# k and v stored by 128-byte pieces after a block transpose, v read back and rounded at half 30, and four steps moved in a one-core hybrid decoder layer

## What is computed

```
h = rms_norm(x) * g_pre
q, k, v, ga, u, vs, gg = split(h @ w_in)          # 512, 256, 256, 512, 512, 512, 512 columns
att = moba(q, k, v, paged cache)                  # 8 heads of 64, 4 kv heads, blocks of 256 keys
v_ln = group_layer_norm(gelu(vs)) * g_sgu
gm = gelu(u) * (tril(w_spatial) @ v_ln + b_spatial)   # chunks of 128 positions
mix = concat(att * silu(ga), gm * silu(gg))
y = x + rms_norm(mix @ w_out) * g_post
```

## Time and profile before

| | |
|---|---|
| median of 3 runs | 285.07 us (284.63, 285.07, 378.24) |
| profiled execution | 283.96 us, of it 282.2 us from the first to the last instruction |
| mean granted TensorE clock | 0.997 of full |
| busy: TensorE, VectorE, ScalarE, GpSimd | 270.9, 197.1, 155.2, 72.3 us |
| DMA | 43.4 MB, 154 GB/s over the span |

### The profile page before, as it was taken

The page is one execution under the profiler, slowest core; times in us unless marked ns, Lnnn a source line. Parts: engine busy times, 40 slices in busy tenths (PEclk is TensorE's granted clock), DMA queues, the critical chain, the costliest instruction groups (busy, mean ns, idle before and its releaser), DMA issues.

```text
span 282.2 us, 6112 instructions
## 1 busy us (share of the span) xinstructions
PE 270.9 (96%) x2155; PEld 238.1 (84%) x2155; DVE 197.1 (70%) x451; ACT 155.2 (55%) x355; POOL 72.3 (26%) x86
## 2 busy tenths in 40 slices
PE   8999989999999999999899999999899999999992
PEld 3799988998997887999687999998799976767892
DVE  4785886598844425925649789899979894927773
ACT  5974578532693323178885466555364562718621
POOL 4546503300311140233033452433450510000000
PEclk9999999999999999999999999999999999999998
DMA  7968997269897888740445017022007504040043
GB/s 244 327 191 209 263 257 175 74 185 277 243 321 226 268 283 246 240 136 16 150 147 162 2 45 217 1 70 82 0 2 266 201 1 151 0 150 2 19 174 123
DMA packets 37602, 43.39 MB, mean 154 GB/s; under 512 B 2963, under 2 KB 32659, under 8 KB 37572
## 3 DMA queue, kind: packets, MB, share of 16 engines
q1 hardware_dynamic: 36626, 40.25, 47.7%
q0 software_dynamic: 944, 2.75, 3.5%
q10 hardware_dynamic: 2, 0.00, 0.0%
HBM read 39.59 MB, written 3.41 MB: 152 GB/s over the span
## 4 chain that ended last, share of the span: by engine, by line
PE 74%; DVE 12%; ACT 9%; issue 3%; DVEq 0%; POOL 0%; ACTq 0%; POOLq 0%
PE Z L1442 11%; PE Z L1447 11%; PE Z L1443 11%; PE T L1360 3%; PE S L1484 3%; DVE probs L1241 3%; PE O L1583 2%; PE Z L1398 2%; PE O L1519 2%; PE S L1398 2%; PE S L1399 2%; PE Z L1400 2%; PE S L1400 2%; PE Z L1399 2%; DVE pT_lo L1247 2%
## 5 line engine op out<-in xcount | busy, mean ns | idle before, releaser
L1442 PE MATMUL Z<-act_hi,w_hi 128*128 128x288 f32 (+1 forms) x344 | 89.6, 293 | 0.4 <-ACT zvs L856 0.3
L1443 PE MATMUL Z<-act_lo,w_hi 128*128 128x288 f32 (+1 forms) x344 | 88.2, 288 | 0.0
L1442 PEld LDWEIGHTS Z<-act_hi,w_hi 128*128 128x128 f32 x344 | 64.8, 188 | 2.6 <-issue 1.6
L1443 PEld LDWEIGHTS Z<-act_lo,w_hi 128*128 128x128 f32 x344 | 64.8, 188 | 0.0
L691 POOL TENSOR_TENSOR w_lo<-w_raw,w_hi 128x1024 fp32r<-128x1024 f32 x16 | 38.2, 2391 | 62.4 <-ACT w_hi L779 62.4
L1447 PE MATMUL Z<-act_hi,w_lo 128*128 128x256 f32 (+1 forms) x336 | 48.9, 288 | 0.0
L1447 PEld LDWEIGHTS Z<-act_hi,w_lo 128*128 128x128 f32 x336 | 44.8, 188 | 0.0
L779 ACT ACTIVATE w_hi<-w_raw 128x1024 fp32r<-128x1024 f32 x32 | 33.6, 1052 | 17.0 <-DMA w_raw<-in_w_out 9.9
L1010 DVE TENSOR_TENSOR w_lo<-w_raw,w_hi 128x1024 fp32r<-128x1024 f32 x15 | 18.1, 1212 | 16.2 <-ACT w_hi L779 16.2
L923 ACT ACTIVATE probs<-S,nmax 128x128 f32<-128x128 f32 (+3 forms) x32 | 16.6, 524 | 22.8 <-DVE nmax L1231 21.5
L1118 DVE STREAM_TRANSPOSE kT<-k_ring 128x1024 f32<-128x1024 f32 x16 | 19.7, 1237 | 0.7 <-PE S L1484 0.5
(11 more groups left out here) (271 smaller groups left out, 549.7 us busy)
## 6 DMA issues: line engine op xcount, KB each, us to landing
w_raw<-in_w_in SPq DMA_DIRECT2D x11, 1024.0 KB, 7.2
k_ring<-in_cache_k SPq DMA_DIRECT2D x64, 128.0 KB, 3.2
v_ring<-in_cache_v SPq DMA_DIRECT2D x64, 128.0 KB, 4.2
w_raw<-in_w_out SPq DMA_DIRECT2D x8, 512.0 KB, 4.4
x_sb<-in_x_prompt SPq DMA_DIRECT2D x4, 512.0 KB, 6.0
x_res<-in_x_prompt SPq DMA_DIRECT2D x4, 512.0 KB, 4.8
out<-y_sb SPq DMA_DIRECT2D x8, 256.0 KB, 2.0
w_raw<-in_w_in SPq DMA_DIRECT2D x2, 512.0 KB, 6.5
```

Of the source, the lines that this page charges most:

```text
L1442: mm(out, wh[:, k, :], act_hi[:, k, cols], start=(k == 0), stop=False)
L1443: mm(out, wh[:, k, :], act_lo[:, k, cols], start=False, stop=False)
```

## The change

- WB goes from half 7 to 8.
- KVN 0 to 3 go, with kvn. In their place VectorE turns kv32 (k0, k1, v0, v1, each 128 channels x 512 tokens) in place by blocks of 32x32 (KVB 0 to 3 at halves 10, 12, 14, 16). GpSimd then stores each by four DMAs of 32 partitions, 512 pieces of 128 bytes each: v at halves 26 and 27 (KVD 2, 3), k at halves 34 and 35 (KVD 0, 1).
- v is read back from its output: GpSimd waits for the eight v stores at half 28 (VLD) and loads 512 KB into v_tok, over the v part of kv32. At half 30 (VST) ScalarE waits for that load and rounds all of it in one copy, VectorE subtracts once. PPV 0 waits for this.
- The first gg tile (VectorE, half 40) waits for all k and v stores.
- VSN 2, 3 and 4 go from halves 28, 29, 31 to 27, 28, 29, LN from half 32 to 30, where it stands behind VST and ahead of DPT 1 and PSC 0.
- At half 43, SP 0 goes behind PSC 13 and PN 13, and PPV 11 ahead of PTR 12.
- SP waits for x tile 1 before it issues x tiles 2 to 4. The first three halves wait for the four parts of act_hi one k-group at a time.

```diff
-    after(7, ("WB",))
+    after(8, ("WB",))
-    after(16, ("KVN", 4), ("KVN", 0))
-    for n, h in enumerate((17, 20, 22)):
-        after(h, ("KVN", 1 + n))
+    for j in range(4):
+        after(10 + 2 * j, ("KVB", j))
+    after(16, ("KVN", 4))
+    after(26, ("KVD", 2))
+    after(27, ("KVD", 3))
+    after(28, ("VLD",))
+    after(30, ("VST",), ("LN",))
+    after(34, ("KVD", 0))
+    after(35, ("KVD", 1))
-    for n, h in enumerate((24, 25, 28, 29)):
+    for n, h in enumerate((24, 25, 27, 28)):
         after(h, ("VSN", n))
-    after(31, ("VSN", 4))
-    after(32, ("LN",))
+    after(29, ("VSN", 4))
@@ schedule(), per half h
+        if spread == [0]:
+            after(h, ("SP", 0), ("PPV", u - 2), ("PTR", u - 1))
+        else:
@@ SyncE
             load_first(1)
+            sp.wait_ge(x_in[1], 16)
             for tt in (2, 3, 4):
@@ GpSimd
+                elif kind == "KVD":
+                    j = s[1]
+                    out, landed = (k_prompt, stored_k) if j < 2 else (v_prompt, stored_v)
+                    rows = out[0, 0].rearrange("(b j) h d -> j b (h d)", j=32)
+                    pool.wait_ge(kv_turned, j + 1)
+                    for a in range(4):
+                        at = P * (j % 2) + 32 * a
+                        pool.dma_start(rows[:, :, at:at + 32], kv32[32 * a:32 * a + 32, j, 0:SEQ].rearrange("p (b i) -> p b i", i=32))\
+                            .then_inc(landed, 16)
+                elif kind == "VLD":
+                    pool.wait_ge(t_full, T_OF["KVN", 4] + 1)
+                    pool.wait_ge(stored_v, 8 * 16)
+                    pool.dma_start(v_tok[:, :, :], v_prompt[0, 0].rearrange("(t p) h d -> p t (h d)", p=P)).then_inc(v_back, 16)
@@ ScalarE
+                elif kind == "VST":
+                    act.wait_ge(v_back, 16)
+                    nc.scalar.activation(v_st[:, :, :, 0:HD], v_tok[:, :, :].rearrange("p t (h d) -> p t h d", h=KVH), ACT.Copy).then_inc(vst_hi, 1)
@@ VectorE
+                elif kind == "KVB":
+                    j = s[1]
+                    if j < 2:
+                        dve.wait_ge(k_first, 2 * j + 2)
+                    else:
+                        dve.wait_ge(z_free["act"], freed(Z_FREED_BY, HALF_AT[TILE_OF["v", j - 2], 1])[1])
+                    nc.vector.transpose(kv32[:, j, 0:SEQ], kv32[:, j, 0:SEQ]).then_inc(kv_turned, 1)
+                elif kind == "VST":
+                    dve.wait_ge(vst_hi, 1)
+                    nc.vector.tensor_tensor(v_st[:, :, :, HD:], v_tok[:, :, :].rearrange("p t (h d) -> p t h d", h=KVH),
+                                            v_st[:, :, :, 0:HD].bitcast(fp32), ALU.subtract).then_inc(vst_done, 1)
@@ TensorE, first three halves
-                        pe.wait_ge(x_hi, 4)
                         for k in range(KD):
+                            if k % 4 == 0:
+                                pe.wait_ge(x_hi, 3 + k // 4)
                             mm(out, wh[:, k, :], act_hi[:, k, cols], start=(k == 0), stop=False)
```

More of the change, by code:

```diff
@@ L125, in schedule @@
         u = h - first
-        if h in [2 * TILE_OF["gg", gp] + 3 for gp in range(3)]:
-            after(h, ("SP", (h - 3) // 2 - TILE_OF["gg", 0]))
+        spread = [gp for gp in range(3) if h == 2 * TILE_OF["gg", gp] + 3]
+        for gp in (spread if spread != [0] else []):
+            after(h, ("SP", gp))
         if u < len(UNITS):
             after(h, ("PSC", u), ("PN", u))
[L130 to L133, removed]
+        if spread == [0]:
+            after(h, ("SP", 0), ("PPV", u - 2), ("PTR", u - 1))
+        else:
+            if 1 <= u < len(UNITS) + 1:
+                after(h, ("PTR", u - 1))
+            if 2 <= u < len(UNITS) + 2:
+                after(h, ("PPV", u - 2))
         after(h, ("ZE", h // 2, h % 2))
@@ L298, in build @@
         R_V = region(4096 + 8192 + 10240)
-        kvn = place("kvn", [P, 2, 512], fp32, R_V)
+        v_tok = place("v_tok", [P, 4, KVW], fp32, R_Z + 2 * ZB + 2 * TOK * 4)
         ln_sq = place("ln_sq", [P, 512], fp32, R_V)
@@ L411, in build @@
         v_in = [sem(f"v_in{n}") for n in range(4)]
-        stored_kv = [sem("stored_kv0"), sem("stored_kv1")]
+        stored_k, stored_v, v_back, kv_turned = (sem(n) for n in ("stored_k", "stored_v", "v_back", "kv_turned"))
         stored_kvs = sem("stored_kvs")
@@ L649, in _ @@
             sp.wait_ge(stored_sgu, 16)
-            for n in range(2):
-                sp.wait_ge(stored_kv[n], 2 * 32)
+            sp.wait_ge(stored_k, 8 * 16)
+            sp.wait_ge(stored_v, 8 * 16)
             sp.wait_ge(stored_kvs, 32)
@@ L729, in _ @@
                 elif kind == "KVN":
[L730 to L731 removed]
                     pool.wait_ge(t_free["act"], freed(T_FREED_BY, T_OF[s])[1])
[L733 to L735 removed]
+                    pool.dma_start(kv_rows(k_prompt, k_sample, 4), kv_s[:, 0:KVW]).then_inc(stored_kvs, 16)
+                    pool.dma_start(kv_rows(v_prompt, v_sample, 4), kv_s[:, KVW:2 * KVW]).then_inc(stored_kvs, 16)
+                elif kind == "KVD":
[11 more added lines that the diff above has]
+                    pool.dma_start(v_tok[:, :, :], v_prompt[0, 0].rearrange("(t p) h d -> p t (h d)", p=P)).then_inc(v_back, 16)
                 elif kind == "DOT" and s[1] == 1:
@@ L872, in _ @@
                     R = ROWS[tt]
[L873 to L880, removed]
+                    take(n, kv_s[:, 0:512], T[n % 2][0:R, :])
+                elif kind == "VST":
+                    act.wait_ge(v_back, 16)
+                    nc.scalar.activation(v_st[:, :, :, 0:HD], v_tok[:, :, :].rearrange("p t (h d) -> p t h d", h=KVH), ACT.Copy).then_inc(vst_hi, 1)
                 elif kind == "DEX":
@@ L1087, in _ @@
                         if what == "gg" and j == 0 and half == 0:
-                            dve.wait_ge(t_full, T_OF["KVN", 3] + 1)
+                            dve.wait_ge(t_full, T_OF["KVN", 4] + 1)
+                            dve.wait_ge(stored_k, 8 * 16)
+                            dve.wait_ge(stored_v, 8 * 16)
                         nc.vector.scalar_tensor_tensor(dst[:, j, cols], th[:, g % 2, 0:wide], 1.0, bank[:, 0:wide], ALU.add, ALU.mult)\
@@ L1573, in _ @@
                     if u == 0:
-                        pe.wait_ge(vst_done, 4)
+                        pe.wait_ge(vst_done, 1)
                         pe.wait_ge(own_taken, 1)
```

4 lines of the change are left out of this document (removed).

## The result

The changed kernel takes 286.71 us (median of 22 executions, 284.55 to 290.76) against 284.36 us for the kernel before, measured beside it (median of 22). The ratio is 1.0077, 95% interval [1.0053, 1.0101]: 0.8% or 2.2 us slower, which is within 2%, but surely not the small gain that was forecast. The medians in this text are of all executions and the ratios leave out those in the slower state, so a difference of medians and one of ratios need not agree.

The account below looks back on a forecast made before the run. TensorE, busy 96% of the span, was taken as the bound. By half 26 -2.7, half 30 +2.2, LN gone -0.45, SP 0 +0.45 sum to -0.5 us: 284.6 us by the median, range 280.5 to 289.5.

Parts of the forecast that it names:

- WB: Half 7 to 8: moving it closes TensorE's 0.82 us wait for VectorE's copy; gain 0.9 us with the restart.
- The sixteen transposes: KVN 0 to 3 removed: four blocks of 0.44 us go and a 0.33 us wait closes; gain 2.1 us.
- KVB: Halves 10 to 16, VectorE: the first block transpose delays the k_lo of half 11; loss 0.3 us, bounds 0 to 0.8.
- The start: Held x tiles and finer wait on act_hi in the first halves: taken 0, bounds -0.3 to +0.3 us.
- The stores and the way back: Halves 26 to 30: 0.75 us an issue, v back near 132.2 just before ScalarE needs it; cost 0.
- Rival 2: v comes back late at VST and TensorE stops: +2.6 us (287.2) to +6 us (290.6); chance 0.17.
- VSN, VST, LN at half 30: Halves 27 to 31: new work ahead of DPT 1 and PSC 0 delays TensorE; loss 2.2 us, upper bound 3.0.
- the collision: Half 30: VectorE's two-input subtraction for v is held by GpSimd's w_lo; half 32 3.0 us late, 2.3 without it.
- LN gone at half 32: Half 32: a table switch goes and TensorE's 0.42 us wait closes; gain 0.45 us.
- SP 0: Half 43: spatial product behind the scores, its sum later on VectorE; taken +0.45 us, between 0.9 lost and nothing.
- rival 3: Order changes in halves 30 and 43 cost their upper bounds, +0.8 and +0.45 us more: 285.9, up to 287; chance 0.10.

Follow-up runs that it names:

- e4: The kernel before with the start alone changed (x tiles held, finer wait, WB at half 8): 283.43 us, ratio 0.9977.
- e6: The kernel before with only the new order of half 43 (spatial product behind scores, product with v ahead of transposes): 286.81 us, ratio 1.0064.
- e11: The kernel before with only the first spatial product moved behind the scores in half 43: 288.24 us, ratio 1.0141.
- e10: The kernel before with only the product with v moved ahead of the transposes of probabilities in half 43: 284.12 us, ratio 0.9998.
- e9: e5 with the four KVB transposes at halves 12, 13, 14 and 16: 282.23 us, ratio 0.9913.
- e1: The changed kernel with x tiles 2 to 4 issued at once, not held: 287.96 us, ratio 1.0151.
- e3: The changed kernel with VSN and LN at their old halves, v still rounded at half 30: 286.10 us, ratio 1.0097.
- e8: The changed kernel with half 43's old order and VSN and LN at their old halves: 284.18 us, ratio 0.9984.
- e14: e2 with VST alone behind the scores and probabilities of head 0 in half 30, LN staying ahead: 283.18 us, ratio 0.9971.
- e5: e2 with VST and LN behind the scores and probabilities of head 0 in half 30: 282.75 us, ratio 0.9913.
- e2: The changed kernel with half 43 in its old order: 283.93 us, ratio 1.0021.

## Why the prediction was wrong, step by step

The forecast was 284.6, a gain of 0.5; the kernel lost 2.2. The range (280.5 to 289.5) and "within 2%" hold. In the profiled executions, without the late load, the sum went from -0.5 to +1.8. Of these 2.3 us half 43 holds 1.96 and half 35, which was not in the sum, 1.12; the start took 0.71 off. By its steps:

- **WB, right.** -0.9 taken, -0.90 measured (e4: 10.34 for 11.24). The wait that it saves is itself not steady: 0.51 in e6, 1.13 in e11 and 1.69 in e10, all with WB at half 7.
- **The sixteen transposes, right.** -2.1 taken, -2.26 measured, and the wait of 0.33 closed.
- **KVB, right.** +0.3 taken, +0.37 measured (0.67 us a transpose for 0.63); e9 confirms its cause, the place ahead of k_lo.
- **The start, 0 taken.** The trace of after shows -0.71, and by e1 the hold of x gains 1.2 us or more in the changed kernel; e4 shows less. The size stays open. The bounds of 0.3 were drawn from one wait (0.70) of one execution, while half 6 alone scatters by 2 us.
- **The stores and the way back, right.** 0.65 us an issue instead of 0.75, no wait at VLD, and ScalarE came to VST at 133.34 with v already there: its load back, issued at 126.61, landed 6.2 us later, 0.5 us ahead. Rival 2 is out. The Trainium skill, DMA: Bandwidth & Descriptors, Specifications, has DMA below 512 bytes read, modify and write; if that happened here it cost no time that a row of after shows. The eight stores of 512 pieces landed 2.6 to 3.8 us after their issues, where the prediction's two packets a piece came to 14.6 us for all eight. In e3, where GpSimd comes to VLD sooner, it waits 0.74 us for them, until 121.40, 3.5 us after the last issue ended.
- **VSN, VST, LN at half 30, right in size, not in its parts.** +2.2 taken, +2.40 measured, at its place and by the collision that the 2.06 us of the earlier trace rows gave reason to expect (2.32 us). But the change of VSN's and LN's halves, to which 1.2 us of lateness were put down, shows no cost once VST stands there (33.87 in e8, 33.85 in e3, 33.92 in after); ScalarE's table load for the second exponential came 0.6 us late, not 1.2 (124.47, 4.95 ahead of half 30's block, where before it was 5.54 ahead). VST's place is enough for the 2.4 (e8), and LN's alone, without VST ahead, costs 1.35 (e14 against e5). What was not in the sum is that the clock falls behind these waits in some executions: half 25 to 32 took 35.25 in e2 and 35.40 in e1, 1.3 to 1.5 more than in after.
- **LN gone at half 32, right, but taken back.** -0.45 taken, -0.66 measured; then +1.12 at half 35 from SyncE's list, which the prediction did not follow: with LN at half 30 the split that the next weight load waits for comes 0.6 late, the v pages behind that load with it, and TensorE, 0.66 early, meets them.
- **SP 0, the step that failed.** +0.45 was taken, halfway between a loss of 0.9 and nothing. The account of VectorE's list in the text was correct, and by it alone the loss is 0.9; the rows of before gave the other end, VectorE early, no weight. With the clock at 1.00 the order costs 1.07 (e3, 13.10 for 12.03), with the clock falling at the wait 2.41 to 2.63 (after, e1, e6). e10 and e11 put the cost on the spatial product behind the scores. The text summed waits and never asked what a wait of 2.3 us does to the clock.

With the measured terms the sum is -0.71 - 0.9 + 0.37 - 2.26 + 2.40 - 0.66 + 1.12 + 2.41 = 1.8 for the profiled execution; by the ratio it is 2.2. So the time is rival 3's, 285.9 to 287, which had been given 0.10, but only half of it for rival 3's reason: the bad order at half 43 did come on top of the collision and went past its upper bound, 2.41 for 0.9, while half 30 stayed near the value taken, 2.40 of at most 3.0, and half 35 is in neither.

## What to carry to other kernels

When a step is moved behind another on TensorE, its tail on VectorE moves behind the other's tail as well; if that tail frees a bank that the next matmuls need, the whole softmax becomes a wait, and two exchanged neighbours must be costed one at a time, up to where the lists meet again (from half 43 to 47 e10 wins 0.13 us, e11 loses 3.46). A new elementwise step belongs behind the ones that TensorE is waiting for, and off the time of GpSimd's two-input work: the same rounding of v cost 2.4 us ahead of the first scores and, with the norm's step behind them too, nothing (from half 25 to 34 44.08 us in e5, 44.33 before). And a new wait of TensorE like these is costed with what the granted clock may take behind it, here another 1.3 to 1.6 us in the executions in which it falls.

## What the runs showed of the hardware

- With a wait of 2.30 us the granted clock was 0.66 over 5 us in after, e1 and e6, and 1.00 in e3, though TensorE was busy 4.08 to 4.10 of the 5 us before that stretch in after, e6 and e3 alike: the price of one and the same wait varies between executions by 1.3 to 1.6 us. The clock fell as well at 1.69 us in e10 and at 1.67 and 0.90 together in e2, and did not at these two in after. Executions of after range from 0.983 to 1.000 in mean clock, while e5's lie between 0.995 and 1.000.
- VectorE's two-input subtraction over 128x1024 took 1.23 us alone and 2.32 us beside GpSimd's (e5 and after; in every trace with the two apart it took 1.23, in every one with them together 2.31 or 2.32), ending 1.1 us after GpSimd's did. The Trainium skill, GPSIMD Engine Reference, Specifications, names the shared port; the trace agrees, with these numbers.
- A DMA of 512 pieces of 128 bytes took GpSimd 0.65 us to issue, between 0.54 for 128 rows and 1.08 for 1024 pieces.
- The third pair of weights, a load of 1 MB in the busiest stretch, comes late in some executions, with the change at the start and without it (half 6 to 9: 10.34 to 15.04 us), by up to 4.7 us with the lower clock behind it. Why it does in one and not in the next was not settled.
